# Keys between the queries: a new order of the operand chunks in a latent-attention layer

## The chip, the cores and the metric

The kernel runs on one core of a Trainium2 chip. Times are microseconds (us) of device time for one launch; the kernel before takes 3174.15 us (median of three runs, 3171.93 to 3174.87). TensorE (PE) multiplies, VectorE (DVE) and ScalarE (ACT) read its results out of the accumulation banks, GpSimd (POOL) makes the low halves of split numbers, and SyncE (SP) issues the transfers. Each engine works through its own queue in program order; a semaphore wait at the head of a queue holds all that stands behind it.

## The reference, cut to what matters

The program is one step of a four-layer encoder (token mixers A, B, C, A) for 1024 prompt tokens and 32 sample tokens; the third layer, C, is the one touched. It is a multi-head latent attention with 12 heads, a query latent `cq` of 384 columns and a key/value latent of 256:

```python
q = (_rmsnorm(cq, q_norm_g) @ w_uq).reshape(B, T, C_HEADS, C_NOPE + C_ROPE)
q_nope, q_rope = q[..., :C_NOPE], _rope(q[..., C_NOPE:], pos)
lat = _rmsnorm(ckv, kv_norm_g)
kv = (lat_all @ w_ukv).reshape(B, lat_all.shape[1], C_HEADS, C_NOPE + C_V)
k_nope, v = kv[..., :C_NOPE], kv[..., C_NOPE:]
s = (einsum(qn, k_nope) + einsum(qr, kr_all)) * scale
p = softmax(where(chunk_mask, s, NEG));  o = einsum(p, v)
```

`lat_all` has 1568 rows (1024 prompt, 32 sample, 512 cached), the queries 1056.

## The kernel before, in words

Every fp32 matrix product is made of three passes over numbers split in a high and a low half (high x high, high x low, low x high). A *job* is one pair of heads; layer C has six, after two jobs for the memory heads. A job has five *units* of queries (`units_of`): groups of 256 prompt queries in the order 1, 2, 0, 3, then the 32 sample queries. They are called unit 0 to unit 4 here. A unit is worked off in *chunks* of keys: 4, 6, 2, 8 and 1 of them.

What is computed inside a unit, in the order of `unit`: for each chunk PE transposes a block of probabilities (`turn`), ACT copies it out rounded (L1062), DVE subtracts to make the low half (L1307), and PE multiplies it with the values (`times_v`, L1593). In chunk 0 stand also the last products of the unit before, its evacuation (ACT L1105, DVE L1334), and the scores of the *next* unit, which PE makes (L1538), DVE adds a mask to (L1278) and ACT takes the exponential of (L1053).

Beside this, each of the first five jobs computes the operands of the *next* job. Each operand is cut into *sides* (chunks of columns that fit one accumulation bank): `uqe` and `uqo`, the queries of the even and the odd head, 3 sides of 352 and 4 of 264 columns with 9 matmuls each; `ck`, the keys of both heads, 4 sides of 392 columns with 6 matmuls; `cv`, the values, 4 like them. So uqe, uqo, ck, cv with a number are used below for single sides. `BESIDE["C"] = (3, 3, 5, 3, 1)` says how many sides stand in each unit: they are taken from one list in its order. In unit 2, with two chunks, three of the five stand in chunk 0 (one ahead of the second tile of the next unit's scores, two behind it), and two in chunk 1.

All sides beside units use one accumulation bank, bank 1. A side's first matmul waits until the side before it has been read (`held_free`). Who reads depends on the operand: DVE reads uqe and uqo in one operation (L1231, multiplying with the rotary table), ACT reads ck in two (L931 and L932, one per head), and cv in one (L945). For the first job there is nothing to hide behind: its 15 sides run in one block, and alternate between two banks.

The weights of a side (`weight`, numbered in the order of their creation) lie in two slots, number modulo 2. When the last side of weight n is done, `used` converts weight n+2 into the same slot (ACT L988 the high half, POOL L1361 the low half) and asks SP to load weight n+4. When all queries and keys of the next job are there, `conv` splits them (ACT L1083, POOL L1394) in unit 3.

Of the kernel before, what the change touches and what calls it, by code (L numbers as in the profile page):

```python
# [170 lines left out]
def units_of(job):  # L171
# [15 lines left out]
OPERANDS = {  # L187
    "M": [("mq", KT, THIRDS)],
    "A": [("q", KT, THIRDS), ("k", KT, THIRDS), ("v", KT, THIRDS)],
    "C": [("uqe", 3, THIRDS), ("uqo", 3, QUARTERS), ("ck", 2, KEY_QUARTERS), ("cv", 2, KEY_QUARTERS)],  # L190
}
OPERANDS["B"] = OPERANDS["A"]

BESIDE = {"M": (1, 1, 1, 0, 0), "A": (2, 1, 3, 2, 1), "B": (2, 1, 3, 2, 1), "C": (3, 3, 5, 3, 1)}


class Plan:
# [67 lines left out]
        return s  # L265

    def operand_sides(self, job, bank_of):
        out = []
        for what, kt, chunks in OPERANDS[job.kind]:
            w = job.operand_weights[what]  # L270
            job.sides[what] = [self.side(w, kt, what, a, n, None, job, c, len(chunks), bank_of(len(out) + c))
                               for c, (a, n) in enumerate(chunks)]
            out += job.sides[what]
        return out

    def part(self, s, part, parts):
# [45 lines left out]
    def stream(self, jobs, late=()):  # L322
# [4 lines left out]
        for j, nxt in zip(jobs, jobs[1:]):  # L327
            count = BESIDE[nxt.kind]
            ends = [sum(count[:i + 1]) for i in range(5)]
# [104 lines left out]
def course():  # L434

    p = Plan()
    w8 = 16
    layers = []
    for layer, kind in enumerate(KINDS):
        x = dict(kind=kind)  # L440
        x["gates"] = [p.weight("w8", w8 + i, KT) for i in range(8)]
        x["mq"] = [p.weight("w8", w8 + 8 + i, KT) for i in range(2)]
        w8 += 10
        if kind == "C":
            x["latents"] = [p.weight("w8", w8 + i, KT) for i in range(6)]
            w8 += 6
            x["pairs"] = [dict(uqe=p.weight("wc_q", 2 * i, 3), uqo=p.weight("wc_q", 2 * i + 1, 3),
                               ck=p.weight("wc_kv", 2 * i, 2), cv=p.weight("wc_kv", 2 * i + 1, 2))
                          for i in range(6)]
        else:  # L450
            x["pairs"] = [{what: p.weight("w8", w8 + 3 * i + c, KT) for c, what in enumerate("qkv")}
                          for i in range(6)]
            w8 += 18
        x["out"] = [p.weight("w8", w8 + i, KT, late=kind == "C" and i < 2) for i in range(KT)]
        w8 += KT
        layers.append(x)
    p.phase("memload", layer=0)
    p.phase("xload")
    p.order += [("wload", 0), ("wload", 1), ("msplit", 0, 0), ("msplit", 0, 1)]
    p.phase("norm", what="mem")  # L460
    p.order += [("mnorm", 0, k) for k in range(KT)] + [("msplit", 0, 2), ("msplit", 0, 3)]
    for t in range(2):
        p.memory(0, t)
    p.split(0)
    for t in range(2, 4):
        p.memory(0, t)
    p.phase("memstore", layer=0)
    p.split(1)
    p.phase("xsum")
    p.phase("norm", what="h", layer=0)  # L470
    p.order += [("hhi", p.n_phases - 1, k) for k in range(KT)]
    for layer, x in enumerate(layers):
        kind = x["kind"]
        memory = [p.job("M", layer, j, 6 + j) for j in range(2)]
        mixers = [p.job(kind, layer, i, i) for i in range(6)]
        for j, w in zip(memory, x["mq"]):
            j.operand_weights = dict(mq=w)
        for j, w in zip(mixers, x["pairs"]):
            j.operand_weights = w
        p.phase("operands", layer=layer, kind=kind)  # L480
        p.order += [("kload", memory[0]), ("vload", memory[0])]
        p.phase("pair", weights=x["gates"][:2], layer=layer)
        p.used(*x["gates"][:2])
        n = 0
        for t, w in enumerate(x["gates"][2:]):
            for c, (a, cols) in enumerate(THIRDS):
                p.part(p.side(w, KT, "gate", a, cols, t, None, c, 3, n % 2), 0, 1)
                n += 1
        p.order.append(("exp_table",))
        for s in p.operand_sides(memory[0], lambda c: c % 2):  # L490
            p.part(s, 0, 1)
        if kind == "C":
            p.stream(memory)
            p.phase("latents", weights=x["latents"])
            n = 0
            for t, w in enumerate(x["latents"]):
                for c, (a, cols) in enumerate(THIRDS):
                    p.part(p.side(w, KT, "latent", a, cols, t, None, c, 3, n % 2), 0, 1)
                    n += 1
            p.phase("latent_cache")  # L500
            p.phase("norm", what="cq")
            p.phase("norm", what="lat")
            p.phase("key_rope")
            for s in p.operand_sides(mixers[0], lambda c: c % 2):
                p.part(s, 0, 1)
            p.stream(mixers, x["out"][:2])
        else:
            p.stream(memory + mixers)
        if layer < DEPTH - 1:
            p.phase("memload", layer=layer + 1)  # L510
        p.phase("out", layer=layer, weights=x["out"])
        p.used(*x["out"][:2])
        p.order += [("square", layer, 0), ("square", layer, 1)]
        for f in range(2, KT):
            p.order.append(("outtile", layer, f, x["out"][f]))
            p.used(x["out"][f])
            p.order.append(("square", layer, f))
            if f < 6 and layer < DEPTH - 1:
                k = 2 * (f - 2)
                p.order += [("msplit", layer + 1, f - 2), ("mnorm", layer + 1, k), ("mnorm", layer + 1, k + 1)]  # L520
        p.order.append(("outsum", layer, 0))
        if layer < DEPTH - 1:
            p.memory(layer + 1, 0)
        p.order.append(("outsum", layer, 1))
        if layer < DEPTH - 1:
            p.phase("norm", what="h", layer=layer + 1)
            ph = p.n_phases - 1
            for t in range(1, 4):
                p.memory(layer + 1, t)
                p.order.append(("hhi", ph, t - 1))  # L530
            p.phase("memstore", layer=layer + 1)
            p.order += [("hhi", ph, k) for k in range(3, KT)]
    p.phase("norm", what="final", layer=DEPTH)
    return p
# [35 lines left out]
def encoder(nc, x_in, mem_in, w8, wc_q, wc_kv, gains_in, lambda_in, rel_in, kcache, vcache, lat_cache,  # L570
# [134 lines left out]
    keys_roped = signal("keys_roped")  # L705

    plan = course()

    out_tile = {w: (m["layer"], f) for t in plan.order if t[0] == "phase" and t[2] == "out"
# [1026 lines left out]
```

## Time and profile before

| | us |
|---|---|
| median of three runs | 3174.15 |
| the profiled execution, as timed | 3170.77 |
| its span, first to last instruction | 3168.8 |
| PE busy | 2797.1 (88%) |
| DVE busy | 1284.6 (41%) |
| ACT busy | 1322.7 (42%) |
| POOL busy | 790.4 (25%) |
| mean granted TensorE clock, share of 2.4 GHz | 0.932 |

The busy times are shares of the whole span, and layer C takes only a part of it: its six head jobs lie between about 1816 and 2330 us. The chain of work that ended last runs over PE for 72% of the span. In rows of the time order, the first number is the start, the second the time until the last of the group ended, then engine, line, operation, result and operands, shape, and count; brackets give the time that the engine stood idle before it and what ended that.

### The profile page before, as it was taken

How to read it: one execution, taken by the hardware profiler on the slowest of the kernel's cores; microseconds unless marked ns; L12 is line 12 of the kernel's file. 1: busy time of each engine (PE TensorE's matmuls, PEld its weight loads, DVE VectorE, ACT ScalarE, POOL GpSimd, SP SyncE). 2: the span in 40 equal slices, each digit the busy share in tenths (PEclk: the TensorE clock that was granted, in tenths of full speed). 3: DMA queues.
4: the chain of work that ended last, by engine and by line, in shares of the span. 5: the costliest groups of instructions: out<-in, count | busy, mean ns of one | idle time of the engine just before them, and what ended most of it. 6: DMA issues, size and time to landing. Idle time of an engine off the chain costs nothing.

```text
span 3168.8 us, 46537 instructions
## 1 busy us (share of the span) xinstructions
PE 2797.1 (88%) x18900; PEld 2620.7 (83%) x18900; DVE 1284.6 (41%) x3173; ACT 1322.7 (42%) x2826; POOL 790.4 (25%) x435
## 2 busy tenths in 40 slices
PE   3989999979989999979988678888789989999987
PEld 3979999969888999879887567777679978999877
DVE  2134555551225656651123144444432035555542
ACT  3234444442234555542232245555533234454431
POOL 3321212205312212205320222221126212222112
PEclk7989999989999999989997889999999989999989
DMA  3111111123111111123110000000042111111111
GB/s 132 44 42 43 51 47 59 47 104 108 46 37 58 48 62 64 61 105 100 54 40 28 24 14 9 7 9 7 14 150 75 49 37 53 46 58 55 41 69 69
DMA packets 58197, 171.59 MB, mean 54 GB/s; under 512 B 6720, under 2 KB 15040, under 8 KB 57472
## 3 DMA queue, kind: packets, MB, share of 16 engines
q1 hardware_dynamic: 57984, 168.62, 15.5%
q8 instruction: 150, 2.46, 0.3%
q14 instruction: 63, 0.52, 0.0%
HBM read 134.67 MB, written 33.92 MB: 53 GB/s over the span
## 4 chain that ended last, share of the span: by engine, by line
PE 72%; ACT 11%; DVE 10%; issue 4%; POOL 2%; DMA 1%; SPq 0%; DVEq 0%; ACTq 0%
PE acc L1517 34%; PE acc L1593 10%; PE acc L1491 9%; PE scores L1538 8%; PE turned L1552 6%; ACT prob L1050 4%; DVE prob L1278 3%; PE scores L1442 2%; DVE raw L1176 2%; POOL h_split L1370 2%; ACT prob L1053 1%; PE scores L1430 1%; DVE y_sb L1334 1%; DVE pt_split L1307 1%; PE turned L1442 1%
## 5 line engine op out<-in xcount | busy, mean ns | idle before, releaser
L1517 PE MATMUL acc<-h_split,w_hi 128*128 128x352 f32 (+1 forms) x4860 | 1214.9, 331 | 73.7 <-ACT w_rest L932 23.5
L1517 PEld LDWEIGHTS acc<-h_split,w_hi 128*128 128x128 f32 x4860 | 854.2, 193 | 101.3 <-ACT w_rest L932 27.5
L1517 PE MATMUL acc<-h_split,w_lo 128*128 128x352 f32 (+1 forms) x2430 | 792.8, 326 | 0.0
L1361 POOL TENSOR_TENSOR w_lo<-w_raw,w_hi 128x1024 fp32r<-128x1024 f32 (+2 forms) x156 | 335.5, 2153 | 1756.0 <-ACT w_hi L988 1756.0
L1278 DVE CUSTOM_DVE_ANT_0 prob<-scores,bias 128x256 f32<-128x256 f32 (+9 forms) x576 | 337.8, 634 | 549.1 <-PE scores L1538 545.7
L1307 DVE TENSOR_TENSOR pt_split<-turned,pt_split 128x512 fp32r<-128x512 f32 (+4 forms) x564 | 303.5, 553 | 590.7 <-ACT pt_split L1062 590.2
L1593 PE MATMUL acc<-pt_split,v_split 128*64 128x256 f32 (+6 forms) x3486 | 501.4, 280 | 26.1 <-ACT pt_split L1062 10.0
L1517 PEld LDWEIGHTS acc<-h_split,w_lo 128*128 128x128 f32 x2430 | 467.9, 193 | 0.0
L1050 ACT ACTIVATE prob<-prob,stat 128x256 f32<-128x256 f32 (+9 forms) x468 | 304.5, 653 | 350.4 <-DVE stat L1278 350.4
L1593 PEld LDWEIGHTS acc<-pt_split,v_split 128*64 128x64 f32 (+2 forms) x3486 | 403.7, 160 | 46.0 <-issue 17.7
L1552 PE MATMUL turned<-ident,prob 128*128 128x128 f32 (+2 forms) x1866 | 289.2, 279 | 92.0 <-DVE prob L1294 46.5
L1062 ACT ACTIVATE pt_split<-turned 128x512 fp32r<-128x512 f32 (+4 forms) x564 | 261.6, 483 | 209.1 <-PE turned L1552 208.1
L1538 PE MATMUL scores<-k_split,q_split 64*128 64x512 f32 (+9 forms) x2196 | 302.7, 358 | 50.7 <-issue 25.8
L1552 PEld LDWEIGHTS turned<-ident,prob 128*128 128x128 f32 (+2 forms) x1866 | 217.3, 145 | 133.0 <-DVE prob L1294 58.3
L1538 PEld LDWEIGHTS scores<-k_split,q_split 64*128 64x128 f32 (+3 forms) x2196 | 205.2, 197 | 102.7 <-issue 50.0
L1491 PE MATMUL acc<-h_split,w_hi 128*128 128x352 f32 x1152 | 280.0, 327 | 9.2 <-POOL w_lo L1361 9.2
L988 ACT ACTIVATE w_hi<-w_raw 128x1024 fp32r<-128x1024 f32 (+2 forms) x156 | 149.9, 965 | 308.2 <-PE acc L1491 200.6
L1491 PEld LDWEIGHTS acc<-h_split,w_hi 128*128 128x128 f32 x1152 | 203.3, 192 | 10.2 <-issue 10.2
L1491 PE MATMUL acc<-h_split,w_lo 128*128 128x352 f32 x576 | 187.2, 325 | 0.0
L1442 PE MATMUL scores<-h_split,w_hi 128*128 128x352 f32 x512 | 130.6, 339 | 31.4 <-POOL h_split L1370 18.1
L1247 DVE TENSOR_TENSOR y_sb<-acc,y_sb 128x352 f32<-128x352 f32 x72 | 37.8, 525 | 244.0 <-PE acc L1491 244.0
L945 ACT ACTIVATE y_sb<-acc 128x352 f32<-128x352 f32 x72 | 33.6, 466 | 238.0 <-PE acc L1517 238.0
(119 smaller groups left out, 2933.9 us busy)
## 6 DMA issues: line engine op xcount, KB each, us to landing
w_raw<-w SPq DMA_DIRECT2D x132, 512.0 KB, 3.7
x_scr<-y_sb SPq DMA_DIRECT2D x24, 528.0 KB, 5.6
y_sb<-x_scr SPq DMA_DIRECT2D x24, 528.0 KB, 7.9
y_sb<-x_in SPq DMA_DIRECT2D x16, 528.0 KB, 10.2
mw_raw<-w SPq DMA_DIRECT2D x16, 512.0 KB, 7.6
bias<-rel_in SPq DMA_DIRECT2D x24, 320.0 KB, 4.2
raw<-kcache SPq DMA_DIRECT2D x18, 256.0 KB, 4.0
v_cache<-vcache SPq DMA_DIRECT2D x18, 256.0 KB, 4.0
```

The source lines that it names most:

```text
L988: act.activation(w_hi[:, n % 2, 0:wide], w_raw[:, n % 2, 0:wide], ACT.Copy).then_inc(whi_made.mark(n), 1)
L1050: act.activation(p, p, ACT.Exp, scale=-1.0, bias=stat[0:tile.rows, i:i + 1], accum_out=stat[0:tile.rows, 8 + i:9 + i]).then_inc(exps_ready ...
L1062: ins = act.activation(pt[0:rows, chunk.p % 2, 0, c0:c0 + n], t_ps[chunk.a % 2][0:rows, c0:c0 + n], ACT.Copy)
L1278: dve.tensor_tensor_reduce(out=prob[0:tile.rows, at:at + tile.width], in0=s_ps[lane][0:tile.rows, tile.at:tile.at + tile.width], in1=bias[ ...
L1307: ins = dve.tensor_tensor(pt[0:rows, chunk.p % 2, 1, c0:c0 + n], t_ps[chunk.a % 2][0:rows, c0:c0 + n], pt[0:rows, chunk.p % 2, 0, c0:c0 + ...
L1361: pool.tensor_tensor(w_lo[:, n % 2, 0:wide], w_raw[:, n % 2, 0:wide], w_hi[:, n % 2, 0:wide].bitcast(F32), ALU.subtract).then_inc(wlo_made ...
L1442: ins = pe.matmul(pair_banks[3 * i + c][:, 0:n], (w_hi, w_lo)[ws][:, w % 2, 128 * k:128 * k + 128], x[:, xs, k, a:a + n], start=k == 0 and ...
L1491: ins = pe.matmul(acc[i % 2][:, 0:n], (w_hi, w_lo)[ws][:, w % 2, 128 * k:128 * k + 128], h_v[:, xs, k, a:a + n], start=k == 0 and y == 0, ...
L1517: ins = pe.matmul(acc[s.bank][:, 0:s.cols], w[ws][:, 128 * k:128 * k + 128], x(xs, k), start=k == 0 and y == 0, stop=k == s.k_tiles - 1 an ...
L1538: ins = pe.matmul(s_ps[lane][0:tile.rows, tile.at + col:tile.at + col + n], q[rows, qs, tile.q0:tile.q0 + tile.rows], k[rows, ks, key:key ...
L1552: ins = pe.transpose(t_ps[chunk.a % 2][0:n, to:to + rows], prob[0:rows, at:at + n], ident[0:rows, 0:rows])
L1593: ins = pe.matmul(acc[0][0:rows, dst:dst + w], values, pt[0:n, chunk.p % 2, ps, src:src + w], start=c == 0 and i == 0 and y == 0, stop=las ...
```

## The change

It puts the sides of layer C in a new order, written out in a table, and creates a job's weights in the order uqe, ck, uqo, cv, so that ck's weight has the other slot than uqe's. The sides of unit 0 were uqe0, uqe1, uqe2 and are uqe0, ck0, uqe1; those of unit 1 were uqo0, uqo1, uqo2 and are uqe2, ck1, uqo0; those of unit 2 were uqo3, ck0, ck1, ck2, ck3 and are ck2, uqo1, ck3, uqo2, uqo3. Units 3 and 4 keep cv0 to cv3. No operation is added or taken away; all sides keep their bank rule and readers.

```diff
+C_ORDER = [("uqe", 0), ("ck", 0), ("uqe", 1), ("uqe", 2), ("ck", 1), ("uqo", 0), ("ck", 2), ("uqo", 1), ("ck", 3),
+           ("uqo", 2), ("uqo", 3), ("cv", 0), ("cv", 1), ("cv", 2), ("cv", 3)]
@@ operand_sides
+        listed = [(what, kt, c, len(chunks), a, n) for what, kt, chunks in OPERANDS[job.kind]
+                  for c, (a, n) in enumerate(chunks)]
+        if job.kind == "C":
+            listed.sort(key=lambda x: C_ORDER.index((x[0], x[2])))
         out = []
-        for what, kt, chunks in OPERANDS[job.kind]:
-            w = job.operand_weights[what]
-            job.sides[what] = [self.side(w, kt, what, a, n, None, job, c, len(chunks), bank_of(len(out) + c))
-                               for c, (a, n) in enumerate(chunks)]
-            out += job.sides[what]
+        for what, kt, c, chunks, a, n in listed:
+            s = self.side(job.operand_weights[what], kt, what, a, n, None, job, c, chunks, bank_of(len(out)))
+            job.sides.setdefault(what, []).append(s)
+            out.append(s)
@@ course
-            x["pairs"] = [dict(uqe=p.weight("wc_q", 2 * i, 3), uqo=p.weight("wc_q", 2 * i + 1, 3),
-                               ck=p.weight("wc_kv", 2 * i, 2), cv=p.weight("wc_kv", 2 * i + 1, 2))
+            x["pairs"] = [dict(uqe=p.weight("wc_q", 2 * i, 3), ck=p.weight("wc_kv", 2 * i, 2),
+                               uqo=p.weight("wc_q", 2 * i + 1, 3), cv=p.weight("wc_kv", 2 * i + 1, 2))
```

The first place is ACT's queue in unit 2, before. `prob` rows are the exponentials of the next unit's two score tiles, `raw_64<-acc` and `w_rest<-acc` the two reads of one ck side, `w_hi` the conversion of a weight (256 columns: ck or cv, 384: uqe or uqo), `pt_split` the copy of transposed probabilities.

```order
L1053 ACTIVATE prob<-prob,stat 128x896 x2
L988 ACTIVATE w_hi<-w_raw 128x256
L1053 ACTIVATE prob<-prob,stat 128x1024 x2
L931 ACTIVATE raw_64<-acc 64x392
L932 ACTIVATE w_rest<-acc 64x392
L931 ACTIVATE raw_64<-acc 64x392
L932 ACTIVATE w_rest<-acc 64x392
L1062 ACTIVATE pt_split<-turned 128x128 x2
L931 ACTIVATE raw_64<-acc 64x392
L932 ACTIVATE w_rest<-acc 64x392
L931 ACTIVATE raw_64<-acc 64x392
L932 ACTIVATE w_rest<-acc 64x392
```

The same place now (the lines of the changed file are six higher):

```order
L1059 ACTIVATE prob<-prob,stat 128x896 x2
L937 ACTIVATE raw_64<-acc 64x392
L938 ACTIVATE w_rest<-acc 64x392
L1059 ACTIVATE prob<-prob,stat 128x1024 x2
L937 ACTIVATE raw_64<-acc 64x392
L938 ACTIVATE w_rest<-acc 64x392
L994 ACTIVATE w_hi<-w_raw 128x256
L1068 ACTIVATE pt_split<-turned 128x128 x2
L994 ACTIVATE w_hi<-w_raw 128x384
```

Two of the four ck reads have left unit 2, one of the two that stay stands ahead of the second exponential, and a weight conversion stands between the last read and the copy.

The second place is DVE's queue in unit 2, before: the mask rows (`prob,stat<-scores,bias`, each with a read of its minimum), and `w_rest<-acc,rope_sb`, the read of a uqo side.

```order
L1341 TENSOR_TENSOR y_sb<-y_sb,recip 128x256
L1231 SCALAR_TENSOR_TENSOR w_rest<-acc,rope_sb 128x264
L1278 ISA prob,stat<-scores,bias 128x1024
L1278 ISA stat 128x1
L1278 ISA prob,stat<-scores,bias 128x1024
L1278 ISA stat 128x1
L1307 TENSOR_TENSOR pt_split<-turned,pt_split 128x128 x2
L1307 TENSOR_TENSOR pt_split<-turned,pt_split 128x512
```

And now:

```order
L1347 TENSOR_TENSOR y_sb<-y_sb,recip 128x256
L1284 ISA prob,stat<-scores,bias 128x1024
L1284 ISA stat 128x1
L1284 ISA prob,stat<-scores,bias 128x1024
L1284 ISA stat 128x1
L1237 SCALAR_TENSOR_TENSOR w_rest<-acc,rope_sb 128x264
L1313 TENSOR_TENSOR pt_split<-turned,pt_split 128x128 x2
L1237 SCALAR_TENSOR_TENSOR w_rest<-acc,rope_sb 128x264 x2
```

The uqo read has moved from ahead of the two mask rows to behind them, and two more stand behind the subtraction.

The third place is ACT's queue in unit 0 of the second job, before (`v_split` is the copy of transposed values):

```order
L1053 ACTIVATE prob<-prob,stat 128x640 x2
L1091 ACTIVATE v_split<-turned 128x8x64
L1053 ACTIVATE prob<-prob,stat 128x768 x2
L1062 ACTIVATE pt_split<-turned 128x512
L1091 ACTIVATE v_split<-turned 128x8x64
L1062 ACTIVATE pt_split<-turned 128x512
L1062 ACTIVATE pt_split<-turned 128x128 x2
```

And now:

```order
L1059 ACTIVATE prob<-prob,stat 128x640 x2
L1097 ACTIVATE v_split<-turned 128x8x64
L1059 ACTIVATE prob<-prob,stat 128x768 x2
L1068 ACTIVATE pt_split<-turned 128x512
L937 ACTIVATE raw_64<-acc 64x392
L938 ACTIVATE w_rest<-acc 64x392
L1097 ACTIVATE v_split<-turned 128x8x64
L1068 ACTIVATE pt_split<-turned 128x512
L1068 ACTIVATE pt_split<-turned 128x128 x2
```

A ck read has moved in between the copy of transposed probabilities and that of transposed values.

## Rows read from the trace of the kernel before

**Rows 1.** Second job: busy us of PE, weight loads, DVE, ACT, POOL; clock; DMA.
```profile
1929.40:2010.40 81.00, 68.11 (x453) 61.04 (x453) 37.26 (x89) 44.56 (x90) 16.51 (x14) 0.94 0.03 9
```
**Rows 2.** Waits of PE over the five jobs: total us, times, longest.
```profile
PE acc L1517 <- ACT w_rest L932: 23.5, 10, 3.6
PE acc L1517 <- ACT raw L945: 8.6, 5, 1.7
```
**Rows 3.** The reads of the sides by line (ns min/median/max).
```profile
L932 ACT ACTIVATE w_rest<-acc x24: 495/495/496, 1840.5 to 2233.0; 64x392 f32<-64x392 f32 x24
L1231 DVE SCALAR_TENSOR_TENSOR w_rest<-acc,rope_sb x24: 423/433/434, 1835.2 to 2217.6; 128x264 f32<-128x264 f32 x24
```
**Rows 4.** Time order, PE, unit 2 of the second job.
```profile
1976.12 0.50 PE L1538 MATMUL scores<-k_split,q_split 128*128 128x512 f32 x1 [1.21 <-DVE stat L1278]
...
1979.01 0.52 PE L1517 MATMUL acc<-h_split,w_hi 128*128 128x392 f32 x2
...
1983.84 1.02 PE L1517 MATMUL acc<-h_split,w_hi 128*128 128x392 f32 x2 [3.61 <-ACT w_rest L932]
...
1985.97 0.63 PE L1552 MATMUL turned<-ident,prob 128*128 128x128 f32 x2
```
**Rows 5.** Time order, ACT, the same stretch.
```profile
1975.08 2.06 ACT L1053 ACTIVATE prob<-prob,stat 128x896 f32<-128x896 f32 x2 [2.40 <-DVE stat L1278]
...
1980.47 2.29 ACT L1053 ACTIVATE prob<-prob,stat 128x1024 f32<-128x1024 f32 x2 [3.03 <-DVE stat L1278]
1982.79 0.49 ACT L931 ACTIVATE raw<-acc 64x392 f32<-64x392 f32 x1
```
**Rows 6.** Time order, DVE, the same stretch.
```profile
1980.35 1.22 DVE L1278 CUSTOM_DVE_ANT_0 prob<-scores,bias 128x1024 f32<-128x1024 f32 x1
```
**Rows 7.** Time order, PE, end of unit 2 and start of unit 3.
```profile
1990.88 0.62 PE L1517 MATMUL acc<-h_split,w_hi 128*128 128x392 f32 x2 [1.09 <-ACT w_rest L932]
...
1992.06 0.60 PE L1552 MATMUL turned<-ident,prob 128*128 128x128 f32 x4
...
1996.17 0.94 PE L1593 MATMUL acc<-pt_split,v_split 128*128 128x256 f32 x6 [0.35 <-issue]
...
1998.92 1.23 PE L1593 MATMUL acc<-pt_split,v_split 128*128 128x256 f32 x6 [0.84 <-ACT pt_split L1062]
2001.86 0.63 PE L1517 MATMUL acc<-h_split,w_hi 128*128 128x392 f32 x2 [1.71 <-ACT raw L945]
```
**Rows 8.** Time order, ACT, the same stretch.
```profile
1993.16 0.51 ACT L988 ACTIVATE w_hi<-w_raw 128x384 fp32r<-128x384 f32 x1
1993.70 0.60 ACT L1062 ACTIVATE pt_split<-turned 128x512 fp32r<-128x512 f32 x1
```
**Rows 9.** Time order, PE, unit 2 of the fifth job.
```profile
2225.12 1.02 PE L1517 MATMUL acc<-h_split,w_hi 128*128 128x392 f32 x2 [3.61 <-ACT w_rest L932]
...
2232.28 0.60 PE L1552 MATMUL turned<-ident,prob 128*128 128x128 f32 x4
```
**Rows 10.** Four stretches, columns as in rows 1; the clock follows POOL.
```profile
1976.00:1980.00 4.00, 3.88 (x18) 3.26 (x18) 1.53 (x5) 1.45 (x3) 0.74 (x1) 1.00 0.15 40
1984.00:1990.00 6.00, 5.79 (x20) 5.22 (x20) 0.49 (x2) 1.61 (x5) 0.00 (x0) 0.53 0.01 3
1921.00:1925.00 4.00, 3.58 (x15) 3.45 (x16) 1.38 (x2) 2.52 (x5) 4.00 (x3) 0.57 0.00 0
2002.00:2006.00 4.00, 3.95 (x30) 3.58 (x30) 1.38 (x2) 3.32 (x6) 4.00 (x4) 1.00 0.00 0
```
**Rows 11.** Time order, units 0 and 1 of the second job.
```profile
1953.62 0.66 PE L1552 MATMUL turned<-ident,prob 128*128 128x128 f32 x4 [1.18 <-DVE pt_split L1307]
...
1962.71 0.66 PE L1564 MATMUL turned<-ident,raw 128*128 128x128 f32 x4 [0.64 <-DVE v_split L1316]
```
**Rows 12.** Time order, start of the first job's block.
```profile
1829.49 0.96 DVE L1231 SCALAR_TENSOR_TENSOR q_even_raw<-acc,rope_sb 128x352 f32<-128x352 f32 x2
1830.07 0.95 PE L1517 MATMUL acc<-h_split,w_hi 128*128 128x352 f32 x2 [8.23 <-DVE q_even_raw L1231]
```

## The prediction

> **What bounds the kernel now.** I read the busy time by stretch first. In a job of the latent layer PE is busy 68.1 of 81 us, DVE 37 and ACT 45 [rows 1]: PE sets the pace, and what can be won lies in the 13 us in which it waits, and in the time it runs at half clock. The list of PE's waits over the five jobs that compute a successor's operands comes next. Its largest entry is 23.5 us in 10 waits, all for ACT's second read of a key side [rows 2]; that is 4.7 us in each job. The reader should see that two very different waits stand in it: one of 3.61 us and one of 1.09 us a job [rows 4, 7, 9].
>
> The time order shows why. In unit 2 before, PE ends ck0 near 1980.2 and cannot start ck1 until bank 1 is read. The read itself takes two operations of 0.495 us [rows 3], but ACT begins it only at 1982.79, since the exponentials of 1024 columns, 2.29 us from 1980.47, stand ahead of it in its queue [rows 5]. ck1 starts at 1983.84 [rows 4]. The 3.61 us are thus 1.0 us of reading and 2.6 us of queue. The 1.09 us between ck2 and ck3 [rows 7] are the read alone.
>
> The clock follows. After the 3.61 us PE runs at half clock, 1.2 GHz: ck1 takes 1983.84 to 1985.97 = 2.13 us [rows 4], where ck3 later takes 1990.88 to 1992.06 = 1.18 us at full clock [rows 7]; the mean granted clock of 1984 to 1990 is 0.53 [rows 10].
>
> **The change part by part.** No work is added, so the sum is over waits. Five jobs repeat each term; I work it out in the second and check it with the fifth.
>
> *Unit 2, the long wait.* Ahead of the second score tile now stands ck2, six matmuls of 392 columns in place of nine of 264 (2352 columns for 2376, the same time). Its read falls to ACT right behind the first exponentials, which end at 1975.08 + 2.06 = 1977.14 [rows 5], so it is over by 1978.2, ahead of 1979.01 when PE wants the bank again [rows 4]. PE then makes uqo1 from 1979.01, about 1.1 us, and ck3 waits for uqo1's read. DVE does that behind its two mask rows of 1024 columns; the second ends at 1980.35 + 1.22 = 1981.57 [rows 6]. The read is 0.43 us [rows 3] and the hand-over 0.05 us (ACT's read ended at 1982.79 + 2 x 0.495 = 1983.78, PE started at 1983.84). So ck3 starts at 1982.05 and not 1983.84: 1.79 us won. A wait of about 1.95 us stays; DVE's mask rows are what is late next.
>
> *Unit 2, the rest.* Before, from the start of ck1 to the end of ck3 it took 1983.84 to 1992.06 = 8.22 us in the second job [rows 4, 7] and 2225.12 to 2232.28 = 7.16 us in the fifth [rows 9]; the fourth goes like the second, the first and third like the fifth, so the mean is 7.58. Now the same stretch holds ck3, the transposes and products of the unit's first chunk, uqo2 and uqo3. At full clock: ck3 1.2; transposes and six products 1.2 (0.94 for such products [rows 7]), under which ACT's read of ck3 is hidden; uqo2 1.1; a wait for its read; uqo3 1.1. That wait is at least the 0.43 us of DVE's read and at most the 1.09 us it replaces. I take 0.7, since DVE must first subtract for the chunk, behind ACT's read, conversion and copy. Sum 5.3 us. If the clock is low for 3.4 us from the start of ck3, it is 6.5 (ck3 2.13, transposes and products 1.5, the rest as before); if it is low throughout, 2.1 + 1.9 + 2.2 + 0.4 + 2.2 = 8.8. The gain is 2.3, 1.1 or -1.2 us.
>
> Which clock? PE waited 1.21 us at 1976 and kept full clock [rows 4, 10]; after 3.61 us it was always low. A remaining wait of 1.95 us is nearest to those for cv's reader, up to 1.7 us [rows 2]: the one that ended at 2001.86 was followed by 1.00 of full clock, the one in 1921 to 1925 by 0.57 [rows 7, 10]. So I take the middle of 2.3 and 1.1: 1.7 us, with -1.2 and 2.3 as ends.
>
> *Start of unit 3.* Before, after ck3's end at 1992.06, ACT reads ck3 (1.0 us) and converts a weight (0.51) before the copy of the new chunk at 1993.70 [rows 8]. Now the last side is uqo3, which DVE reads; ACT has only the conversion to do, so the copy can begin at the transposes' end, 0.65 after uqo3, instead of 1.64. ACT's evacuation, the next exponentials and the next copy follow it in the queue, all about 1.0 earlier. PE's waits of 0.35 and 0.84 us there [rows 7] add to 1.19; I take 1.0 of it, ends 0 and 1.19. The wait of 1.71 for cv0's reader stays, since ACT's splits stand ahead of it as before.
>
> *Units 0 and 1.* They receive ck0 and ck1, so ACT gets 0.99 us of reading in each, and the conversion of uqo's weight moves into unit 1 (0.51, in place of one as long elsewhere). In unit 0 the read stands behind the copy whose subtraction ends PE's wait of 1.18 us [rows 11], so that wait does not grow; what is queued behind the read is the copy of transposed values, which PE needs only two transposes later. Unit 0's matmuls get 0.4 us shorter (2352 columns for 3168), which goes into that wait; unit 1's get as much longer, and find 0.64 us of wait to fill [rows 11]. ck1's read pushes one copy back, by less than its own length. I take a loss of 0.2 us, ends 2.0 (both reads fully exposed) and a gain of 0.4.
>
> *The first job's block.* PE waits there 8.23 us for DVE, which ropes the keys before it reads uqe0 at 1829.49 [rows 12]. PE now has uqe0 and ck0 to do in front of that wait, 0.4 to 0.8 us less work than uqe0 and uqe1, and that much more behind it. Then keys and queries alternate over two banks, so ACT's 1.0 us of reading has 2 us of room, and short waits between key sides mostly go. But uqo's weight may be converted only after uqe2, with ck1 alone for cover (0.51 us on ACT, POOL's half after it, beside 1.1 to 2.1 us of matmuls). I take 0, ends -1.2 and +1.5 us.
>
> *Weights.* SP's loads keep their distance: each is issued two conversions ahead, and the queue holds in this layer nothing else that waits. In the streamed jobs uqo's conversion has ck1's two chunks as cover, cv's two uqo sides. Nothing.
>
> *Sum.* 1.79 + 1.7 + 1.0 - 0.2 = 4.3 us a job, 21.5 us in five. Against the profiled execution's 3170.8 (span 3168.8 and 2 around it) that is 3149.3. The median of the runs shown, 3174.15, lies 3.4 above that execution, so the forecast for a median is 3152.6, rounded to 3153.
>
> **A rule that speaks against it.** After the change all sides beside units still use bank 1, and the wait left at ck3 is one for that bank's reader, as is the 3.61 us [rows 4]. The Trainium skill, Perfetto Trace Analysis, section Optimizing Tensor Performance, Matmuls, says that independent groups of matmuls should rotate through banks, so that the evacuation of one lies beside the next one's matmuls. By that rule a new order in one bank wins nothing in itself, and the sum would be 0; by the rows it wins what ACT's queue adds to the reading, 2.6 of 3.61 us [rows 4, 5].
>
> **The rivals.**
>
> *The waits only move.* Every side still waits for the reader of the one before, and a reader that is late at one place is late at another: DVE, behind 2.4 us of mask rows, could hold ck3 as long as ACT did. For it speaks that bank 1 is unchanged. Against it: row by row DVE is free 1.8 us before ACT was [rows 5, 6]. If units 0 and 1 gave that back, the time stays at 3174.
>
> *The clock stays low.* PE's waits in unit 2 shrink, but 1.21 and 1.95 us close together hold the clock at half through ck3, uqo2 and uqo3. Then the second term is -1.2: 1.79 - 1.2 + 1.0 - 0.2 = 1.4 a job, 7 in five, 3167. For it: 1921 to 1925 after a shorter wait [rows 10]. Against it: 2002 to 2006.
>
> *Slower: ACT paces units 0 and 1.* If the moved reads do stand in front of what PE waits for, its wait of 1.18 us there becomes 2.17, and so in unit 1; then each may be followed by half clock, as the 3.61 us was, for 5.6 us or more of 6 [rows 10], 2.8 to 3.4 us lost each. 2 x 0.99 + 2 x 3.4 = 8.8 a job, less 4.5 won in units 2 and 3, is 4.3, or 21 in five: 3195. It decides from 5.8 us a job lost. Against it stands the queue order: the copy that PE's transposes wait for is ahead of the read.
>
> **How the numbers follow.** Forecast 0.79, with its own range 3145 to 3160; clock low 0.10; waits only move 0.06; ACT paces 0.05. About 0.2% (6.3 us) is what can be told from no change here. Faster: 0.79 and six of the ten hundredths of the clock rival, 0.85; same: the other four and 0.06, 0.10; slower 0.05. The upper end, 3166, takes in most of the clock rival; the lower, 3143, is the sum of the good ends (1.79 + 2.3 + 1.19 + 0.4 = 5.7 a job, 28, and the block's 1.2, with a little of the second term's clock elsewhere).
>
> **What would show it.** Right: no wait of 3.6 us for `w_rest` by ACT in unit 2, instead five waits near 2 us for DVE's read; the jobs' distance, some 80 us, falls to about 76; PE's waits of 0.35 and 0.84 at unit 3's start gone; waits in units 0 and 1 unchanged. Wrong: new waits for ACT's L937/L938 in units 0 or 1, a conversion of uqo's weight ending a wait of PE, or half clock in unit 2 of all five jobs.

## The result and the profile after

The changed kernel takes 3154.77 us (median of five runs, 3152.46 to 3157.51), the kernel before 3171.93 beside it: a ratio of 0.9948 (95% interval 0.9936 to 0.9959), 17 us less. A second set on another occasion gave 0.9932 (0.9919 to 0.9945), 3152.96 against 3173.22, 20 us less. The forecast was 3153 us, 21.5 us less.

The head of the page after: PE's busy time is the same as before, the span 18.4 us shorter.

```profile
span 3150.4 us, 46537 instructions
PE 2796.6 (89%) x18900; PEld 2619.0 (83%) x18900; DVE 1284.8 (41%) x3173; ACT 1319.8 (42%) x2826; POOL 789.9 (25%) x435
```

What PE waited for over the five jobs, now (total us, times, longest), to set beside [rows 2]:

```profile
PE acc L1523 <- DVE w_rest L1237: 11.2, 10, 1.7
PE acc L1523 <- ACT raw L951: 8.5, 5, 1.7
...
PE acc L1599 <- ACT pt_split L1068: 3.1, 7, 0.7
PE acc L1523 <- ACT w_rest L938: 0.8, 5, 0.2
```

The 23.5 us for ACT's key reads have become 0.8, and 11.2 us for DVE's query reads have come in. In the second job's unit 2, PE in order of time (start, until the last ended, line, operation; in brackets the idle time before and its releaser), to set beside [rows 4, 7]:

```profile
1971.93 0.50 PE L1544 MATMUL scores<-k_split,q_split 128*128 128x512 f32 x1 [1.24 <-DVE stat L1284]
...
1977.79 0.63 PE L1523 MATMUL acc<-h_split,w_hi 128*128 128x392 f32 x2 [1.71 <-DVE w_rest L1237]
...
1980.22 0.52 PE L1523 MATMUL acc<-h_split,w_hi 128*128 128x264 f32 x2 [0.16 <-ACT w_rest L938]
...
1982.09 0.51 PE L1523 MATMUL acc<-h_split,w_hi 128*128 128x264 f32 x2 [0.53 <-DVE w_rest L1237]
...
1983.29 0.60 PE L1558 MATMUL turned<-ident,prob 128*128 128x128 f32 x4
...
1989.17 1.23 PE L1599 MATMUL acc<-pt_split,v_split 128*128 128x256 f32 x6 [0.44 <-ACT pt_split L1068]
1992.10 0.69 PE L1523 MATMUL acc<-h_split,w_hi 128*128 128x392 f32 x1 [1.71 <-ACT raw L951]
```

Two engines' rows say what ended these waits. DVE, where the read of uqo1 stands behind the mask row that ends at 1977.38 (answer to [rows 6]):

```profile
1976.16 1.22 DVE L1284 CUSTOM_DVE_ANT_0 prob<-scores,bias 128x1024 f32<-128x1024 f32 x1
1977.30 0.08 DVE L1284 DVE_READ_ACCUMULATOR2_ANT stat<- 128x1 f32 x1
1977.30 0.43 DVE L1237 SCALAR_TENSOR_TENSOR w_rest<-acc,rope_sb 128x264 f32<-128x264 f32 x1
```

and ACT (answer to [rows 5, 8]), which reads ck2 ahead of the large exponentials, and after uqo3 has only a conversion to do before the copy of unit 3:

```profile
1972.98 0.49 ACT L937 ACTIVATE raw<-acc 64x392 f32<-64x392 f32 x1
1973.48 0.49 ACT L938 ACTIVATE w_rest<-acc 64x392 f32<-64x392 f32 x1
1976.28 2.30 ACT L1059 ACTIVATE prob<-prob,stat 128x1024 f32<-128x1024 f32 x2 [2.30 <-DVE stat L1284]
...
1983.55 0.53 ACT L994 ACTIVATE w_hi<-w_raw 128x384 fp32r<-128x384 f32 x1 [2.60 <-PE acc L1523]
1983.98 0.58 ACT L1068 ACTIVATE pt_split<-turned 128x512 fp32r<-128x512 f32 x1
```

To see where the time went I cut each job at two marks that both kernels have: the start of the second score tile in unit 2 (1976.12 before, 1971.93 now) and the start of cv1 in unit 3, after the 1.71 us wait for ACT's read of cv0 (2001.86 before, 1992.10 now). The stretch between them, five times: before 24.54, 25.74, 24.66, 25.77 and 24.27 us, now 20.20, 20.17, 20.20, 20.19 and 20.16. That is 4.8 us less a job. The rest of a job, from the second mark to the first of the next, went the other way. Before (start and end, length, then the busy us of PE, weight loads, DVE, ACT and POOL; the number behind these five is the clock):

```profile
1921.42:1976.12 54.70, 50.12 (x349) 46.22 (x349) 29.16 (x72) 28.66 (x61) 11.82 (x9) 0.94 0.02 7
2001.86:2057.07 55.21, 50.02 (x348) 46.19 (x348) 29.24 (x72) 28.65 (x61) 11.82 (x9) 0.94 0.02 7
2081.73:2136.41 54.68, 50.09 (x349) 46.26 (x349) 29.15 (x72) 28.66 (x61) 11.82 (x9) 0.94 0.02 7
2162.18:2217.39 55.21, 50.02 (x348) 46.20 (x348) 29.24 (x72) 28.65 (x61) 11.81 (x9) 0.94 0.01 4
```

and now:

```profile
1915.85:1971.93 56.08, 51.41 (x339) 47.20 (x339) 28.38 (x70) 30.66 (x65) 11.80 (x9) 0.91 0.03 7
1992.10:2047.15 55.05, 50.22 (x339) 45.59 (x340) 28.38 (x70) 30.48 (x65) 11.80 (x9) 0.94 0.03 7
2067.35:2124.57 57.22, 52.63 (x340) 48.53 (x340) 28.47 (x70) 30.66 (x65) 11.77 (x9) 0.89 0.02 7
2144.76:2200.91 56.15, 51.51 (x339) 47.25 (x339) 28.38 (x70) 30.65 (x65) 11.78 (x9) 0.91 0.01 4
```

The mean is 54.95 us before and 56.13 now, 1.2 us more. The length follows the clock: where it is 0.94 as before, the stretch takes 55.05, as before; each 0.02 to 0.03 of it costs 1.1 us. ACT's busy time there rose by 2.0 us (the two reads), and PE's time not busy is the same, 4.6 to 4.8 us where it was 4.6 to 5.2: the reads themselves are hidden.

So the five stretches won 24.1 us and the four between them lost 4.7. Three more parts of the head jobs lost time in this execution. The first job's block, from PE's first side (1816.22, now 1812.18) to its first scores (1856.31, now 1852.75), takes 40.57 instead of 40.09 us. From there to the first mark, which is units 0 and 1 of the first job, it takes 42.90 instead of 40.57, at a clock of 0.89 instead of 0.96. And from the fifth mark to PE's first product behind the head jobs it takes 91.47 instead of 85.45. PE stands idle there for 18.2 us where it was 20.0, but the clock is lower:

```profile
2241.66:2327.11 85.45, 65.42 (x441) 57.70 (x442) 41.48 (x98) 45.60 (x90) 14.82 (x9) 0.90 0.11 35
2221.07:2312.54 91.47, 73.29 (x441) 65.04 (x442) 41.49 (x98) 45.50 (x90) 14.79 (x9) 0.80 0.10 32
```

The first is before, the second now. All head jobs together take 500.36 us where they took 510.89, only 10.5 less. In the profiled execution of the second set the last part takes 87.78, and all together 496.77, 14.1 less than before. The rest of the shorter spans, 7.8 and 8.7 us, lies ahead of the block and behind the head jobs, where the change moved nothing. The ten traces of this document have 1811.2 to 1816.2 us ahead of the block and 837.9 to 844.0 behind the head jobs, and both traces of the changed kernel lie near the lower end of each. Whether this belongs to the changed kernel or to these two executions, no run here shows.

### The profile page after: what moved, and what is told of

Same layout as the page of the kernel before. It is cut to its first block, busy times and chain, and to the rows that moved or that the text cites. A ratio compares the mean times of both kernels' runs of the same rounds, so it can differ in the third digit from the quotient of the medians.

```text
span 3150.4 us, 46537 instructions
## 1 busy us (share of the span) xinstructions
PE 2796.6 (89%) x18900; PEld 2619.0 (83%) x18900; DVE 1284.8 (41%) x3173; ACT 1319.8 (42%) x2826; POOL 789.9 (25%) x435
## 4 chain that ended last, share of the span: by engine, by line
PE 74%; ACT 10%; DVE 9%; issue 4%; POOL 3%; DMA 1%; SPq 0%; DVEq 0%; ACTq 0%
PE acc L1523 36%; PE acc L1599 10%; PE acc L1497 9%; PE scores L1544 8%; PE turned L1558 6%; ACT prob L1056 3%; PE scores L1448 2%; DVE prob L1284 2%; DVE raw L1182 2%; POOL h_split L1376 2%; PE scores L1436 1%; PE turned L1448 1%; DVE pt_split L1313 1%; DVE y_sb L1340 1%; ACT prob L1059 1%
## 5 line engine op out<-in xcount | busy, mean ns | idle before, releaser
L1523 PE MATMUL acc<-h_split,w_hi 128*128 128x352 f32 (+2 forms) x4860 | 1207.7, 330 | 63.5 <-POOL w_lo L1367 18.5
L1523 PE MATMUL acc<-h_split,w_lo 128*128 128x352 f32 (+2 forms) x2430 | 788.5, 324 | 0.0
```

What stands on the lines that cost most here:

```text
L1523: ins = pe.matmul(acc[s.bank][:, 0:s.cols], w[ws][:, 128 * k:128 * k + 128], x(xs, k), start=k == 0 and y == 0, stop=k == s.k_tiles - 1 an ...
```

## The experiments

All were timed beside the kernel before, with four to eleven executions of each, in two groups of four that shared a chip. The first group asks where the gain comes from, the second what is left. The changed kernel itself was timed again in the second group only; the first group is set against the 17 and 20 us that it won beside the kernel before. Median of before: 3169.29 us in the first group, 3173.22 in the second.

**The weights' order alone.** The changed kernel with the old list in the table:

```diff
-C_ORDER = [uqe0, ck0, uqe1, uqe2, ck1, uqo0, ck2, uqo1, ck3, uqo2, uqo3, cv0, ...]
+C_ORDER = [uqe0, uqe1, uqe2, uqo0, uqo1, uqo2, uqo3, ck0, ck1, ck2, ck3, cv0, ...]
```

> Only the weights come in the order uqe, ck, uqo, cv; the sides stand in the old order. Theory of places (the gain comes from which reader stands where in unit 2): no gain, 0 to 3 us slower than before, about 3173 us, since in the first block uqo's weight is now converted right after uqe2 with nothing between; PE's wait of 3.6 us for ACT's second ck read stays in all five jobs. Rival (the earlier conversions win): 3155 us, like the changed kernel.

Measured: 3188.14 us, ratio 1.0059 (1.0046 to 1.0071), 19 us slower, so both expectations missed, mine in size. In the first block PE waits twice for a weight's low half, and the 3.61 us in unit 2 are there as before (the last line):

```profile
1834.45 0.81 PE L1523 MATMUL acc<-h_split,w_hi 128*128 128x264 f32 x2 [1.76 <-POOL w_lo L1367]
1848.00 0.63 PE L1523 MATMUL acc<-h_split,w_hi 128*128 128x392 f32 x2 [2.20 <-POOL w_lo L1367]
...
1911.86 1.02 PE L1523 MATMUL acc<-h_split,w_hi 128*128 128x392 f32 x2 [3.61 <-ACT w_rest L938]
```

The block takes 46.1 us, 6.0 more. The stretch between the marks stays at 24.5 to 25.6 us. Most of what is left comes from the clock: the rest of three jobs runs at 0.88 and takes 57.35 us, here one of them, and the part behind the fifth mark takes 89.86, 4.4 more than before:

```profile
2009.55:2066.90 57.35, 52.85 (x348) 49.04 (x348) 29.23 (x72) 28.59 (x61) 11.80 (x9) 0.88 0.02 7
```

So the weights' order by itself is no gain: with the old list it costs 19 us, and with the new list the block loses 0.5. The new list with the old order of weights was not run. The run also shows that the clock can take 2.4 us a job without any new wait there.

**ck2 behind the second score tile.** The changed kernel with two entries exchanged:

```diff
-... ("uqo", 0), ("ck", 2), ("uqo", 1), ("ck", 3), ...
+... ("uqo", 0), ("uqo", 1), ("ck", 2), ("ck", 3), ...
```

> The changed kernel with uqo1 and ck2 exchanged in unit 2: uqo1 stands ahead of the second score tile, ck2 and ck3 behind it. Theory of places (ACT's queue of exponentials makes the long wait): the 3.6 us wait for ACT's read is back between ck2 and ck3, 1.9 us more a job than the 1.71 now, with half clock behind it 1 to 2 us more: 10 to 16 us of the gain are lost, 3164 to 3170 us. Rival (mixing readers wins because fewer ck sides are neighbours): one more neighbouring ck pair costs its read less DVE's, 0.6 us a job, 3 us: 3158 us.

Measured: 3167.43 us, ratio 0.9992 (0.9983 to 1.0001): nearly all of the gain is gone, as the theory of places said (3164 to 3170), and not the 3158 of the rival. The wait is back to the hundredth, and ACT's rows show its cause:

```profile
1980.16 2.29 ACT L1059 ACTIVATE prob<-prob,stat 128x1024 f32<-128x1024 f32 x2 [3.33 <-DVE stat L1284]
1982.47 0.49 ACT L937 ACTIVATE raw<-acc 64x392 f32<-64x392 f32 x1
1982.98 0.49 ACT L938 ACTIVATE w_rest<-acc 64x392 f32<-64x392 f32 x1
1983.52 1.02 PE L1523 MATMUL acc<-h_split,w_hi 128*128 128x392 f32 x2 [3.61 <-ACT w_rest L938]
```

Between the marks it takes 23.0 us in four jobs, 2.8 more than the changed kernel: 1.9 of wait, the rest the half clock behind it (1.02 us for two matmuls, against 0.63). Against the kernel before, 2.0 us a job are still won between the marks in these four jobs, yet the whole time hardly shows them: the rests take 55.6 to 55.9 us where before has 54.95, and units 0 and 1 of the first job 42.9, as in the changed kernel.

**ck3 last in unit 2.**

```diff
-... ("ck", 2), ("uqo", 1), ("ck", 3), ("uqo", 2), ("uqo", 3), ("cv", 0), ...
+... ("ck", 2), ("uqo", 1), ("uqo", 2), ("uqo", 3), ("ck", 3), ("cv", 0), ...
```

> The changed kernel with ck3 last in unit 2 (ck2, uqo1, uqo2, uqo3, ck3). Theory: the 1.71 us wait for DVE stays, but ACT again reads a key side and converts a weight in front of unit 3's first copy, so PE's waits of 0.35 and 0.84 us at its start come back: 1.0 us a job, 5 us, 3160 us; wait between uqo3 and ck3 0.5 us as now. Rival (the last reader does not matter, all comes from the long wait): 3155 us.

Measured: 3157.23 us, ratio 0.9964 (0.9951 to 0.9976), 12 us less than before, where the changed kernel has 17 and 20. The waits at unit 3's start are back (0.24 and 0.84 us, once 0.35 and 0.84), those in unit 2 unchanged:

```profile
1980.65 0.51 PE L1523 MATMUL acc<-h_split,w_hi 128*128 128x264 f32 x2 [1.71 <-DVE w_rest L1237]
1984.56 0.63 PE L1523 MATMUL acc<-h_split,w_hi 128*128 128x392 f32 x2 [0.53 <-DVE w_rest L1237]
1989.74 0.95 PE L1599 MATMUL acc<-pt_split,v_split 128*128 128x256 f32 x6 [0.24 <-issue]
1992.49 1.22 PE L1599 MATMUL acc<-pt_split,v_split 128*128 128x256 f32 x6 [0.84 <-ACT pt_split L1068]
```

Between the marks it takes 20.6 us, only 0.45 more than the changed kernel, since with uqo2 right behind uqo1 the wait of 0.16 us for ck3's read is gone. So the last reader matters, by some 0.5 us net in this order, half of the 1.0 expected; the whole time's difference of 5 to 8 us also has the block's in it (42.9 us, 2.3 more, since cv's weight is converted late there, a wait of 2.19 us for POOL). By the ratio, 0.9964 of 3171.93, the time comes to the 3160 us expected, but partly by luck, since the expectation had no such term.

**The moved reads doubled.** To see whether units 0 and 1 have room, ACT makes two more copies there, to an unused place:

```diff
+                if job.index and s.chunk < 2:
+                    for i in range(2):
+                        act.activation(w_rest[64:128, 2 * s.chunk + i, Q_LORA:Q_LORA + CHUNK_KEY], src[64:128, 0:s.cols], ACT.Copy)
                 act.activation(raw[1][0:64, cols], src[0:64, 0:s.cols], ACT.Copy)
```

> The changed kernel with two more copies of half a ck side (2 x 0.49 us on ACT, to an unused place) ahead of the read of ck0 and ck1, in the jobs whose operands are made beside units. Theory (the moved reads are hidden in units 0 and 1, and what the rest of the job loses, about 1.2 us, is half clock that falls elsewhere): 0 to 3 us more than the changed kernel, 3155 to 3158 us. Rival (the moved reads stand in PE's way in units 0 and 1): 0.6 us per us added as now, or all of it: 1.2 to 2 us a job, 6 to 10 us more, 3161 to 3165 us.

Measured: 3159.99 us, ratio 0.9970 (0.9961 to 0.9979), 9 us less than before, so 8 to 11 of the gain lost; I had expected 0 to 3, the rival 6 to 10. PE now waits for the key read in unit 1:

```profile
1968.58 0.48 PE L1526 MATMUL acc<-h_split,w_hi 128*128 128x264 f32 x2 [0.93 <-ACT w_rest L941]
```

The time in which PE stands idle in the rest of a job rises from 4.6 to 4.8 us to between 5.9 and 6.7. Of the 1.97 us added, some 1.1 to 2.1 come up as idle time; the first reads, without the copies, added none. The rests themselves are only 0.7 us longer than in the changed kernel (56.80 in the mean), since the clock was higher in two of the four; two neighbours:

```profile
1920.76:1976.74 55.98, 49.25 (x339) 44.38 (x340) 28.38 (x70) 32.30 (x69) 11.83 (x9) 0.97 0.02 7
1996.96:2054.53 57.57, 51.64 (x339) 47.30 (x339) 28.37 (x70) 32.47 (x69) 11.80 (x9) 0.91 0.03 7
```

The room in units 0 and 1 was there for the moved reads, and 0.98 us more for each side is too much: the rival's view of these units is wrong for the change and right for its double.

**Second group.** The changed kernel again, as the yardstick:

> The changed kernel once more, as the yardstick for the three others. Theory: 17 us under the kernel before on the same chip (ratio 0.9946), from five stretches of unit 2 and the start of unit 3 that are 4.8 us shorter each, less about 1.2 us a job of half clock that falls elsewhere; the half-clock time between two such stretches 7 to 13 us a job where before had 6.8. Rival (that extra half clock was a chance of one execution): 6.8 us in every job, and a ratio of 0.993.

Measured: 0.9932, 3152.96 us. Its trace repeats the first: 20.16 to 20.22 us between the marks, and 56.07, 55.10, 57.15 and 56.18 us in the rest. The extra half clock of these four stretches is thus no chance of one execution, but belongs to the kernel. Behind the fifth mark the two executions differ (91.47 and 87.78 us). The ratio itself favours the rival's 0.993 over the theory's 0.9946, which lies just outside the interval (0.9919 to 0.9945); it is the trace that speaks against the rival.

**The splits of unit 3 in halves.** Two of ACT's four operations in each of chunks 1 to 4, in place of four in chunks 1 and 3 (the engines' programs take the half as a last number of the item):

```diff
+                if at == 3 and following is not None and following.kind == "C":
+                    if c <= 4:
+                        order.append(("conv", following, (c - 1) // 2, (c - 1) % 2))
-                if at == 3 and following is not None and c in (1, 3 if n > 4 else 2):
+                elif at == 3 and following is not None and c in (1, 3 if n > 4 else 2):
```

> The changed kernel, with the splitting of the next job's operands in unit 3 (four operations of ACT, 2.97 us, ahead of cv0's read) cut in halves, two operations in each of four chunks. Theory (the 1.71 us wait for cv0's reader is ACT's queue, and the half clock behind it follows from that wait): wait falls to about 0.3, half clock between two stretches to at most 6.8 us a job; 1.4 + 0 to 1.7 us a job, 7 to 14 us less than the changed kernel. Rival (PE then waits as long for the next copy of probabilities behind the split): same time as the changed kernel, 2 us either way.

Measured: 3142.81 us, ratio 0.9899 (0.9885 to 0.9913), 10 us less than the changed kernel, within the theory's 7 to 14. The wait of 1.71 us is 0.42, with a second like it for cv1's reader:

```profile
1988.92 0.63 PE L1530 MATMUL acc<-h_split,w_hi 128*128 128x392 f32 x2 [0.42 <-ACT raw L954]
1994.59 0.62 PE L1530 MATMUL acc<-h_split,w_hi 128*128 128x392 f32 x2 [0.43 <-ACT raw L954]
```

and the clock in the rest of the job is back at 0.94, once 0.97 (two of the four stretches; this execution took 3135.61 us, 7 less than the median of its five):

```profile
1914.52:1969.99 55.47, 50.48 (x339) 45.88 (x339) 28.47 (x70) 31.65 (x67) 13.14 (x10) 0.94 0.02 7
1988.92:2043.12 54.20, 49.10 (x340) 44.38 (x340) 28.39 (x70) 31.67 (x67) 13.15 (x10) 0.97 0.02 7
```

**Four sides in unit 1, four in unit 2.**

```diff
-... ("ck", 2), ("uqo", 1), ("ck", 3), ("uqo", 2), ("uqo", 3), ...   "C": (3, 3, 5, 3, 1)
+... ("ck", 2), ("ck", 3), ("uqo", 1), ("uqo", 2), ("uqo", 3), ...   "C": (3, 4, 4, 3, 1)
```

> The changed kernel with four sides in unit 1 (uqe2, ck1, uqo0, ck2) and four in unit 2 (ck3 | uqo1, uqo2, uqo3): only one side stands behind the second score tile, and the transposes and products of the next chunk come before the following one. Theory (what is left of the long wait is DVE's read behind two mask rows): wait of 1.71 falls to about 0.6, that of 0.53 stays; 1.1 us a job, 5.5 us less than the changed kernel. Rival (ACT has no room for a third key read in units 0 and 1, as the doubled reads cost about 2 us of waits a job): new waits for L938 in unit 1 of 0.5 to 1 us a job, 0 to 2 us more or less than the changed kernel.

Measured: 3145.25 us, ratio 0.9907 (0.9894 to 0.9921), 8 us less than the changed kernel. Only one side stands behind the score tile, and the wait of 1.71 us has become 0.79, the next 0.82 instead of 0.53:

```profile
1978.72 0.51 PE L1523 MATMUL acc<-h_split,w_hi 128*128 128x264 f32 x2 [0.79 <-DVE w_rest L1237]
1980.89 0.52 PE L1523 MATMUL acc<-h_split,w_hi 128*128 128x264 f32 x2 [0.82 <-DVE w_rest L1237]
```

Between the marks it takes 18.05 us, 2.1 less; half of that is a side that unit 1 now makes. No wait for a key read came up in unit 1. The waits for bank 1 fell by 0.8 us a job, less than the 1.1 expected, and the whole time by more than the 5.5 expected; where the difference comes from is not shown.

**Both.**

> conv_halves and four_four together. Theory: the two gains add, 12 to 18 us less than the changed kernel, 0.989 of the kernel before. Rival (one wait takes the other's place): no better than the better of the two.

Measured: 3136.74 us, ratio 0.9882 (0.9867 to 0.9897), 36 us less than before and 16 less than the changed kernel: the two gains nearly add (10 + 8), and this is the fastest version. What PE still waits for bank 1 beside the units (total us, times, longest):

```profile
PE acc L1530 <- DVE w_rest L1242: 8.0, 10, 0.8
PE acc L1530 <- ACT raw L954: 4.3, 10, 0.4
```

## Why the prediction was right, point by point

- *The long wait.* Forecast 1.79 us, from DVE's mask rows in place of ACT's queue. From the score tile's start to ck3 it took 5.86 us, where ck1 had taken 7.72: 1.86. The wait left was 1.71, forecast 1.95. The exchange of two entries brought it back; shown.
- *The rest of unit 2.* Forecast 1.7, between half and full clock. It ran at full clock in all five jobs: 5.50 to 5.53 us from ck3 to uqo3's end, where before it was 7.58 in the mean: 2.1. My full-clock sum was 5.3.
- *Start of unit 3.* Forecast 1.0. From the last side's end to cv1's mark 8.81 us, before 9.80 (in the fifth job 9.38): 0.99 in four jobs and 0.6 in the fifth, though the wait of 0.84 has gone only to 0.44.
- *Units 0 and 1.* Forecast a loss of 0.2; no idle time of PE was added. But the doubled reads show that 0.98 us more a side is too much for ACT there, which I had not worked out.
- *The block.* Forecast 0, measured 0.5 us of loss. The wait for uqo's weight that I had bounded is 0.69 us, and PE's wait for DVE grew by the same 0.7 that its work in front of it shrank. A wait of PE that a conversion of uqo's weight ends was on the prediction's list of signs that it is wrong; it came up in the block alone, and in no job that is made beside units:

```profile
1826.03 0.96 PE L1523 MATMUL acc<-h_split,w_hi 128*128 128x352 f32 x2 [8.91 <-DVE q_even_raw L1237]
...
1833.29 0.51 PE L1523 MATMUL acc<-h_split,w_hi 128*128 128x264 f32 x2 [0.69 <-POOL w_lo L1367]
```

- *What the sum lacked.* The three terms of units 2 and 3 came to 4.5, measured 4.8: the mechanism held, and the distance from one job to the next, 79.2 to 81.0 us before, is now 75.2 to 77.4, forecast about 76. The clock in the rest of the job, which I had left as it was, took back 1.2 us a job, and in the first trace 2.3 us in units 0 and 1 of the first job and 6.0 behind the fifth mark. I had weighed the clock only where the waits changed. It fell in places whose waits had not changed; the halves of the splits took a wait away there, and the clock was higher again. Why it falls after one wait of 1.71 us and not after another in the same place stays open: the two traces of the changed kernel share their pattern up to the fifth mark and part behind it, the other kernels have patterns of their own, and no run here told what sets it.
- *What was luck.* The sum of 21.5 us lies close to the 17 and 20 measured, closer than its terms deserve. It counted five times 4.3 us and nothing else. In the two traces the head jobs gave 10.5 and 14.1 us, because the clock took back much of 24.1, and 7.8 and 8.7 us came from parts that the sum did not touch.
- *The rule on rotating banks.* The prediction took from the Trainium skill (Perfetto Trace Analysis, section Optimizing Tensor Performance, Matmuls) that independent groups of matmuls should rotate through banks, and worked out from it a gain of 0. All sides stayed in one bank, and yet 4.8 us a job were won there: of the 3.61 us, 2.6 were not the reading but what stood ahead of the reader in its queue. That does not refute the rule, since no run here gave the sides a second bank. The waits for bank 1 that are left in the fastest version, 0.4 and 0.8 us each, are one to two readings long (0.43 us on DVE, 0.50 on ACT), and a second bank might win some of them.

## What to carry to other kernels

When PE waits for a bank's reader, compare the wait with the reading's own duration: what is over it is queue, and the same bank with another engine's reader, or the same reader two places earlier, got most of it back here without another bank. Place a read ahead of the long operation of its engine, not behind it, and cut an engine's long groups where PE's next read stands behind them. Count the half clock over the whole loop, since it can move to stretches that were not touched.

## What the runs showed that I had not expected

The same instructions with nearly the same waits (PE idle for 4.6 to 4.8 us) took 55.05 to 57.22 us, depending on how much of the stretch ran at half clock (mean granted clock 0.94 to 0.89); in the kernel with the old list it was 57.35 at 0.88. And an order of weights that had looked neutral cost 19 us: 6.0 in one block, where PE waited 4.0 us for conversions, and most of the rest in the clock.
